# VectorE makes the whole low half of every weight unit and the whole rotary product; GpSimd keeps only the power in the norms

## What is computed

```python
# first block
u = rms_norm(h, mix_pre_gain)
b_gate, c_gate, v_a, val_b, gate_b = split(u @ w_in)
y_a = b_gate * causal_dwconv(c_gate * v_a, conv_a_w)          # 3 taps
g = causal_dwconv(val_b * sigmoid(gate_b), conv_b_w) + bias   # 31 taps
y_b = silu(layer_norm(g))
h = h + rms_norm(concat(y_a, y_b) @ w_out)
h = h + rms_norm(square(relu(rms_norm(h) @ w_up)) @ w_down)
# second block, layer A
u, gate = split(rmsnorm(x) @ w_in_a)
x = x + (einsum(pool(u), w_grp) * scale * silu(gate)) @ w_out_a
k = rope(rmsnorm(x, norm_kv) @ w_k);  v = rmsnorm(x, norm_kv) @ w_v
# layer B: 3 groups of queries with dilated windows, 16 heads of 128
q_g = rope(hdn @ w_q[g]); out_g, lse_g = dilated_window_attention(q_g, k, v)
x = x + (softmax_over_groups(lse) * out summed * silu(gate)) @ w_out_b
out = rmsnorm(x)
# rope: t1, t2 = halves of 128;  concat(t1*cos - t2*sin, t2*cos + t1*sin)
```

## Time and profile before

| | us |
|---|---|
| median of 3 runs | 2249.6 (2247.55 to 2251.31) |
| profiled execution | 2251.88, its span 2249.0 |
| TensorE busy | 2092.0 (93%) |
| VectorE busy | 1488.1 (66%) |
| ScalarE busy | 963.1 (43%) |
| GpSimd busy | 930.1 (41%) |
| read from memory | 378.20 MB, 170 GB/s over the span |

### The profile page before, as it was taken

One profiled execution on the slowest core, in us unless ns is written; L12 is line 12 of the kernel. 1 busy time (PEld: TensorE's weight loads), 2 busy tenths in 40 slices (PEclk: granted clock), 3 DMA queues, 4 the chain that ended last, 5 costly groups with the idle time before them and its releaser, 6 DMA issues.

```text
span 2249.0 us, 29026 instructions
## 1 busy us (share of the span) xinstructions
PE 2092.0 (93%) x11160; PEld 1799.1 (80%) x11160; DVE 1488.1 (66%) x1813; ACT 963.1 (43%) x1226; POOL 930.1 (41%) x531
## 2 busy tenths in 40 slices
PE   6867699999999999999999998989999989989998
PEld 6756587788888888888878887878888878778887
DVE  4999975466465565565466865348726888888763
ACT  4232244444444444444445455434443434434542
POOL 5554447430000000000446475636766545545663
PEclk9988899999999999999999999999999999999999
DMA  6443337466665656656645565644565443444563
GB/s 210 134 127 115 113 115 235 161 209 207 192 191 187 192 191 188 190 187 186 195 136 175 168 206 165 228 151 150 198 195 183 136 141 122 149 133 131 169 245 129
DMA packets 305864, 384.29 MB, mean 171 GB/s; under 512 B 11673, under 2 KB 237209, under 8 KB 303936
## 3 DMA queue, kind: packets, MB, share of 16 engines
q1 hardware_dynamic: 305536, 382.22, 53.6%
q10 hardware_dynamic: 192, 0.23, 0.0%
HBM read 378.20 MB, written 4.19 MB: 170 GB/s over the span
## 4 chain that ended last, share of the span: by engine, by line
PE 70%; DVE 21%; issue 3%; ACT 3%; DMA 2%; POOL 0%; DVEq 0%; SPq 0%; ACTq 0%; POOLq 0%
PE job_banks L473 25%; PE job_banks L475 13%; PE job_banks L512 9%; PE job_banks L514 9%; PE job_banks L513 9%; DVE wide_rows L1176 7%; DVE weights_low L1093 3%; PE aux_banks L688 2%; ACT weights_high L751 2%; DVE value L1109 1%; DVE scratch L1440 1%; DMA raw_weights<-in_w_in 1%; DVE scratch L1443 1%; DVE scratch L1439 1%; DVE wide_rows L1135 1%
## 5 line engine op out<-in xcount | busy, mean ns | idle before, releaser
L1571 POOL TENSOR_TENSOR weights_low<-raw_weights,weights_high 128x512 fp32r<-128x512 f32 (+2 forms) x480 | 871.0, 1831 | 1212.1 <-ACT weights_high L751 1210.8
L1093 DVE TENSOR_TENSOR weights_low<-raw_weights,weights_high 128x512 fp32r<-128x512 f32 (+2 forms) x696 | 722.9, 1049 | 579.7 <-ACT weights_high L751 578.6
L751 ACT ACTIVATE weights_high<-raw_weights 128x1024 fp32r<-128x1024 f32 x696 | 725.3, 1055 | 677.9 <-PE job_banks L514 271.7
L473 PE MATMUL job_banks<-act_a,weights_high 128*128 128x512 f32 (+1 forms) x2688 | 909.9, 393 | 73.6 <-DVE value L1109 56.9
L475 PE MATMUL job_banks<-act_a,weights_low 128*128 128x256 f32 (+1 forms) x2624 | 723.2, 277 | 0.0
L473 PEld LDWEIGHTS job_banks<-act_a,weights_high 128*128 128x128 f32 x2688 | 516.3, 194 | 182.3 <-DVE weights_low L1093 60.7
L475 PEld LDWEIGHTS job_banks<-act_a,weights_low 128*128 128x128 f32 x2624 | 512.0, 195 | 0.3
L473 PE MATMUL job_banks<-act_b,weights_high 128*128 128x512 f32 x1088 | 392.4, 403 | 6.5 <-DVE value L1109 6.5
L475 PE MATMUL job_banks<-act_b,weights_low 128*128 128x256 f32 x1088 | 306.0, 281 | 0.0
L473 PEld LDWEIGHTS job_banks<-act_b,weights_high 128*128 128x128 f32 x1088 | 206.6, 190 | 55.6 <-DVE weights_low L1093 8.2
L512 PE MATMUL job_banks<-weights_high,act_b 128*128 128x512 f32 x608 | 238.1, 392 | 1.6 <-DVE act_b L1116 1.6
(11 more groups left out here) (122 smaller groups left out, 1366.6 us busy)
## 6 DMA issues: line engine op xcount, KB each, us to landing
raw_weights<-in_w_up SPq DMA_DIRECT2D x128, 512.0 KB, 3.8
raw_weights<-in_w_down SPq DMA_DIRECT2D x128, 512.0 KB, 4.3
raw_weights<-in_w_in_b SPq DMA_DIRECT2D x128, 512.0 KB, 4.2
raw_weights<-in_w_in SPq DMA_DIRECT2D x80, 512.0 KB, 3.6
raw_weights<-in_w_in_a SPq DMA_DIRECT2D x64, 512.0 KB, 4.7
raw_weights<-in_w_out SPq DMA_DIRECT2D x32, 512.0 KB, 4.8
raw_weights<-in_w_out_a SPq DMA_DIRECT2D x32, 512.0 KB, 4.4
raw_weights<-in_w_k SPq DMA_DIRECT2D x32, 512.0 KB, 4.5
```

The costliest lines, as they stand in the source:

```text
L473: made = e.matmul(o_both, wh[:, k, cols], rhs, start=opens, stop=False)
L751: e.activation(high[:, s, :], raw[:, r, :], ACT.Copy).then_inc(*high_done.inc(n))
L1093: e.tensor_tensor(low[:, s, cols], raw[:, r, cols], high[:, s, cols].bitcast(F32), ALU.subtract).then_inc(*low_done.inc(n))
L1571: e.tensor_tensor(low[:, s, cols], raw[:, r, cols], high[:, s, cols].bitcast(F32), ALU.subtract).then_inc(*low_done_pool.inc(n))
```

## The change

GpSimd no longer makes any part of a low half, and no cosine product. VectorE makes all 1024 columns of each low half in one instruction, and in `rotate` first multiplies `value` by the cosines into `partial`, then goes on as before. TensorE and SyncE wait for `low_done` alone. The order of everything else is unchanged; VectorE waits once for the rotary tables, before the keys.

```diff
-        low_done_pool = signal("low_done_pool")
-        cos_done = signal("cos_done")
...
-        def cut_of(n):
-            if n < convolving:
-                return UNIT // 8
-            if from_grp <= n < to_grp:
-                return UNIT // 4
-            return UNIT if from_up <= n < to_down else UNIT // 2
...
                     if n >= RAW_SLOTS:
-                        before = n - RAW_SLOTS
-                        e.wait_ge(*low_done.at(before))
-                        if cut_of(before) < UNIT:
-                            e.wait_ge(*low_done_pool.at(before))
+                        e.wait_ge(*low_done.at(n - RAW_SLOTS))
...
-            def weights_there(n):
-                e.wait_ge(*low_done.at(n))
-                if cut_of(n) < UNIT:
-                    e.wait_ge(*low_done_pool.at(n))
...
-                weights_there(n)
+                e.wait_ge(*low_done.at(n))
...
             def low_of(n):
                 if n >= total:
                     return
-                r, s, cols = n % RAW_SLOTS, n % SPLIT_SLOTS, slice(0, cut_of(n))
+                r, s = n % RAW_SLOTS, n % SPLIT_SLOTS
                 e.wait_ge(*high_done.at(n))
-                e.tensor_tensor(low[:, s, cols], raw[:, r, cols], high[:, s, cols].bitcast(F32),
+                e.tensor_tensor(low[:, s, :], raw[:, r, :], high[:, s, :].bitcast(F32),
                                 ALU.subtract).then_inc(*low_done.inc(n))
...
             def rotate(event, job, dst):
                 v, part = value_of(job), part_of(job)
                 e.wait_ge(*gathered.at((job.id, 0)))
+                e.tensor_tensor(part, v, cos, ALU.mult).then_inc(*rotated.inc((event, "cos")))
                 e.tensor_tensor(dst[0:mid], v[mid:P], sin[mid:P], ALU.mult).then_inc(*rotated.inc((event, "a")))
                 e.tensor_tensor(dst[mid:P], v[0:mid], sin[0:mid], ALU.mult).then_inc(*rotated.inc((event, "b")))
                 e.wait_ge(*rotated.at((event, "b")))
-                e.wait_ge(*cos_done.at(event))
                 e.tensor_tensor(dst, dst, part, ALU.add).then_inc(*rotated.inc(event))
...
         def gpsimd(e):
-            def low_of(n):
...
+            e.memset(minus_half[:, :], -0.5).then_inc(*half_made.inc("half"))
+            e.wait_ge(*half_made.at("half"))
+            for name, half in (("mix", 0), ("mix", 1), (("up", "post"), 0), ("up", 0), (("up", "post"), 1), ("up", 1),
+                               (("pool", "post"), 0), ("pool", 0), (("pool", "post"), 1), ("pool", 1),
+                               ("keys", 0), ("keys", 1), ("final", 0), ("final", 1)):
                 e.wait_ge(*mean_square.at((name, half)))
                 e.tensor_tensor(rstd[:, half:half + 1], sumsq[:, half, 7:8], minus_half[:, 0:1], ALU.pow).then_inc(
                     *rstd_made.inc((name, half)))
```

More of the change, by code:

```diff
@@ L292, in build @@
         total = len(units)
-        convolving = mix_a[-1].last + 1
-        from_up, to_down = up[1][0].at, down[SUPERS - 2][2].at
-        from_grp, to_grp = grp[0][0].at, proj_a[0].at
-        def cut_of(n):
-            if n < convolving:
-                return UNIT // 8
-            if from_grp <= n < to_grp:
-                return UNIT // 4
-            return UNIT if from_up <= n < to_down else UNIT // 2
         bufs = {"a": act_a, "b": act_b}
@@ L1453, in norm_queries @@
                 yield from turned("queries", half, "b", 1)
+            e.wait_ge(*const_ready.at("consts"))
             run_all(norm_keys(1, 0))
@@ L1565, in gpsimd @@
         def gpsimd(e):
-            def low_of(n):
-                if n >= total or cut_of(n) == UNIT:
-                    return
-                r, s, cols = n % RAW_SLOTS, n % SPLIT_SLOTS, slice(cut_of(n), UNIT)
-                e.wait_ge(*high_done.at(n))
-                e.tensor_tensor(low[:, s, cols], raw[:, r, cols], high[:, s, cols].bitcast(F32),
-                                ALU.subtract).then_inc(*low_done_pool.inc(n))
-            def units_of(job):
-                for n in range(job.at, job.last + 1):
-                    low_of(n + SPLIT_SLOTS)
-            def inverse_root(name, half):
+            e.memset(minus_half[:, :], -0.5).then_inc(*half_made.inc("half"))
[3 more added lines that the diff above has]
+                               ("keys", 0), ("keys", 1), ("final", 0), ("final", 1)):
                 e.wait_ge(*mean_square.at((name, half)))
```

56 lines of the change are left out of this document (1 added, 55 removed).

## The result

The changed kernel takes **2138.5 us** (median of 4 runs, 2136.6 to 2140.0) against 2249.9 us before, beside it on the same chip: ratio 0.9501, with an interval of 0.9489 to 0.9512. The gain is 111 us. The forecast was 2165 us, a gain of 85, with a range of 2145 to 2195 us.

What follows compares the result with a forecast made beforehand. VectorE was taken to bound the convolution and cause TensorE's attention waits, partly standing still beside GpSimd's reads. Terms 1.5 + 46 + 5 + 7 - 1.6 + 27 = 85 us gave 2165 us, range 2145 to 2195.

Steps and rivals of the forecast that it cites:

- Rival C: Long steps are VectorE's own and do not go with GpSimd; slower, 2299 us; chance 0.04.
- Rival B: Loading binds the convolution instead; half of its 46 us is lost, 2188 us; chance 0.09.
- the forecast of 46 us: Convolution, 56 to 280 us: VectorE stays the bound, its saving is the saving; bounds 38 and 50.
- The loss of 38.5 us: Convolution: added cost of 52 full low halves; by a skill page's first half alone, about 2288 us.
- the attention's term: Queries and attention, 1710 to 2100 us: four fifths of TensorE's waits go, 27 us, between 10 and 35.
- the second wait: Attention: TensorE's 14.8 us called "issue", scoring a batch's second head waits for VectorE's split of its first.
- rival A: The attention keeps its waits; only a quarter of the 33 us goes, 2184 us; chance 0.13.
- 3 + 2 + 2 = 7 us: Gain at three turns between stages, near 440, 1170 and 1500 us; bounds 1 and 13.
- The start: Kernel start: VectorE makes the first low parts faster than GpSimd; gain 1.5 us, between 0 and 3.
- The grouped projection: Near 1380 us, eight one-unit jobs: longer low half, shorter product, about +0.2 us a job, costing 1.6 us.
- The layer norm: 280 to 337 us: full low halves no dearer, other two-operand instructions freed; gain 5 us, between 1 and 10.
- The far end of 2207 us: Slow end of the first forecast's times, 2141 to 2207, if all terms' bounds fell together.

Runs made afterwards that it cites:

- GpSimd's needless subtractions: Changed kernel, with GpSimd subtracting a constant tile from itself, unread, in place of each old low part and cosine product; 2353.7 us, ratio 1.0454.
- the cosine products alone: Kernel before, with only the 32 cosine products moved to VectorE and GpSimd keeping its share of every low half; 2232.9 us, ratio 0.9923.

## Why the prediction was right, and where it was not

*The mechanism was right.* Long steps stand beside GpSimd's reads and go with them; the convolution's end came at 230.9 us (forecast near 232), the step's mean is 479 ns (0.47), the low half's over the whole kernel 1223 ns (1.226), GpSimd is busy 8.0 us (about 8), VectorE 1438.8 us (some 1440). Rival C, that the long steps are VectorE's own, is wrong: they came back with GpSimd's needless subtractions. Rival B, that loading binds the convolution, did not happen: 155 GB/s were moved from 56 to 231 us, against 123 before, and ScalarE waited less for loads. In the convolution the forecast of 46 us, VectorE's saving less the price of the full low halves, gave 44.8. The loss of 38.5 us that the prediction set against this (about 2288 us) did not come.

*The step that failed is the attention's term: "27 us, between 10 and 35 (the upper one adds the matmuls that ran at a lower clock)".* It measured 46.3 us, above its own upper bound, and 19 of the 26 us by which the sum is short are here. Two things in it were off. I took four fifths of the waits as gone, and all went: the second wait, whose slack I put at 0.6 us, vanished, so that rival A has nothing for it. That is 28.8 us instead of 27, a small matter. (One wait of 2.6 us stays, in the last batch behind the stretch.) The large one is the clock. I had read the stretch's mean of 0.96 and valued it at 2 us, by the step from 33 to 35. The trace of before could have given more: six scoring groups behind waits took 23.3 us together where six undisturbed ones of 2.17 take 13.0, which is 10 us for these matmuls alone, and some of those behind them were slow as well. Measured over the same matmuls, the term is 28.8 us of idle time and 15.0 of clock; the last 2.6 or so of the 46.3 came just behind the stretch.

*"3 + 2 + 2 = 7 us" for the three turns:* the first two gave 3.5 and 2.1 us. The last, with the keys, gave 7.9. From the mean square of the keys' second half (at 1507.0 us before, 1448.5 after) to the rotation that begins the attention's stretch, TensorE stood idle for 3.9 us before and stands for 1.1 after, and was busy 202.2 us against 198.5: of 6.5 us there, 3.7 are clock again. This is a second step that failed: I had put no term on the keys, writing that the granted clock is at full speed there by slices; the slice's digit of 9 hid a mean of 0.98.

*The start* gave 4.0 us, not 1.5, over its bound of 3. *The grouped projection* cost 2.7 us with the stage before it, not 1.6. The loop itself came out as forecast: its products follow each other every 4.02 us before and 4.20 after, 0.18 us a job. The rest was lost before it and behind it, and was not taken apart. *The layer norm* gave 5.4 us (5).

*The range* failed with the clock: its low end of 2145 us rested on an attention of at most 35 us. With the attention at its measured 46 us and the other terms as forecast, the sum is 85 + 19 = 104 us and the time 2146, just inside it. The far end of 2207 us was added up wrong: the lower bounds of the terms sum to 48 us, which gives about 2202. The range did not rest on it.

## What to carry to other kernels

Look in the timeline for a VectorE instruction with two operands in SBUF that is longer than its like beside a reading GpSimd instruction (11.38 us for 2.05 here): such busy time is standing still, and moving that work from GpSimd to a busier VectorE can lower even VectorE's busy time (by 49 us here, with 480 larger instructions). Where TensorE waits often and shortly, count more than the waits' length: compare one group of matmuls behind a wait and without one, and the clock in the stretch behind it; in these kernels a wait or pause of 3 us or more was followed by 1.5 to 3 us of lost clock, whatever its length up to 6.7 us. When taking out a stall or adding filler work to any engine, look at what small, urgent instruction stands in that engine's in-order queue.

## What was not expected of the hardware

- A pause of TensorE of 3.3 us and one of 6.7 us cost the same behind them, 2.0 and 2.1 us. One of 2.09 us brought the granted clock to 0.56 for 3.85 us, and one of 2.22 us, 20 us ahead of it, did not. With the cosine products alone, of two waits of 2.78 us one cost the clock. What decides it there stays open.
- The rotary cosine product is nearly free on GpSimd once the low halves are gone (2139.8 against 2138.5 us), though it doubles one VectorE product (1573 against 688 ns).
- With GpSimd busy for 1225.9 us, nearly all of it with memsets, VectorE's instructions with two large operands kept their durations (479 and 1223 ns), but 24 `TENSOR_SCALAR` instructions with one became longer (352 to 414 ns in the changed kernel, 607 to 654 here). With a quarter of the memsets the program stayed within 4 us.
